# Rounded weights by a casting transfer on GpSimd's queue, in place of a multiply on GpSimd

## What is computed

```
h = rmsnorm(x, norm_w[l])
proj = jnp.einsum("bsd,de->bse", h, w_in[l])                  # 2048 -> 6160, l = 0, 1
... ssd_branch, conformer_branch, diff_attention_branch ...
x = x + jnp.einsum("bse,ed->bsd", y, w_out[l])                # 2048 -> 2048
...
z = u @ w_in                                                  # 2048 -> 9216, second block
... dilated_band_attention, hgrn2_direction, both ways ...
h = h + rmsnorm_2(y, g_post)                                  # y after @ w_out, 2048 -> 2048
gate = jax.nn.sigmoid((h @ w_pg).astype(f32))                 # 2048 -> 2048
```

## Time and profile before

| | |
|---|---|
| time, median of 3 runs | 3098.46 us (3096.57 to 3101.62) |
| span of the profiled execution | 3093.4 us |
| TensorE busy | 2997.9 us, 97% of the span |
| GpSimd busy | 1976.8 us, 64% |
| VectorE, ScalarE busy | 1750.6 us, 1000.6 us |
| bytes moved | 298.68 MB, mean 97 GB/s |

### The profile page before, as it was taken

How to read it: one execution, slowest core, us unless ns; L and a number is a source line. 1 busy time by engine, 2 the same in 40 slices (tenths; PEclk the granted TensorE clock), 3 DMA queues, 4 the chain that set the end, 5 groups by cost and what they waited for, 6 DMA issues and landing times.

```text
span 3093.4 us, 39590 instructions
## 1 busy us (share of the span) xinstructions
PE 2997.9 (97%) x15236; PEld 2355.2 (76%) x15236; DVE 1750.6 (57%) x2350; ACT 1000.6 (32%) x1712; POOL 1976.8 (64%) x1860
## 2 busy tenths in 40 slices
PE   8999999999999999999999999999999999899997
PEld 6887777788778878777877777777777777687686
DVE  7745887751374569777217443334788778801412
ACT  6243223330233331334103232233544454411422
POOL 6665676577676656756757655555567777566364
PEclk9999999999999999999999999999999999999998
DMA  5322222233223222222432222222212222232122
GB/s 210 110 102 103 82 93 84 82 142 123 99 106 109 102 86 90 97 82 75 172 109 97 84 86 70 83 72 77 79 69 83 73 80 81 93 133 98 66 89 89
DMA packets 59340, 298.68 MB, mean 97 GB/s; under 512 B 6512, under 2 KB 7408, under 8 KB 29200
## 3 DMA queue, kind: packets, MB, share of 16 engines
q1 hardware_dynamic: 36960, 251.67, 23.1%
q10 hardware_dynamic: 22192, 44.48, 4.2%
HBM read 274.04 MB, written 16.84 MB: 94 GB/s over the span
## 4 chain that ended last, share of the span: by engine, by line
PE 74%; DVE 16%; ACT 4%; POOL 3%; issue 2%; DMA 1%; ACTq 1%; DVEq 0%; POOLq 0%
PE bank L433 65%; POOL w_lo L2595 2%; DVE rec_ex L2432 1%; DVE rec_cum L2297 1%; PE bank L777 1%; POOL w_hi L2593 1%; ACT att_sc L1322 1%; PE bank L786 1%; PE bank L794 1%; DMA w_raw<-in_wall 1%; DVE newton L1796 1%; DVE newton L1798 1%; DVE bank L1899 1%; DVE att_sc L2173 1%; PE bank L966 1%
## 5 line engine op out<-in xcount | busy, mean ns | idle before, releaser
L433 PE MATMUL bank<-h_hi,w_lo 128*128 128x512 f32 x3712 | 1501.6, 405 | 24.7 <-POOL w_lo L2595 14.8
L433 PE MATMUL bank<-h_hi,w_hi 128*128 128x512 f32 x3712 | 1453.0, 391 | 0.0
L433 PE MATMUL bank<-h_lo,w_hi 128*128 128x512 f32 x3712 | 1451.5, 391 | 0.0
L2593 POOL TENSOR_SCALAR w_hi<-w_raw 128x512 fp32r<-128x512 f32 x928 | 705.3, 760 | 1004.0 <-PE bank L433 913.0
L2595 POOL TENSOR_TENSOR w_lo<-w_raw,w_hi 128x512 fp32r<-128x512 f32 x928 | 1294.0, 1394 | 77.4
L433 PEld LDWEIGHTS bank<-h_hi,w_lo 128*128 128x128 f32 x3712 | 700.6, 189 | 230.4 <-issue 52.2
L433 PEld LDWEIGHTS bank<-h_hi,w_hi 128*128 128x128 f32 x3712 | 700.1, 189 | 150.9
L433 PEld LDWEIGHTS bank<-h_lo,w_hi 128*128 128x128 f32 x3712 | 701.7, 189 | 146.2 <-issue 10.5
L1034 ACT ACTIVATE raw<-bank 128x512 f32<-128x512 f32 x148 | 88.5, 598 | 403.9 <-PE bank L433 366.3
L2098 DVE SCALAR_TENSOR_TENSOR bank<-cfm_up,par,bank 128x512 f32<-128x512 f32 x232 | 175.4, 756 | 8.3
L1805 DVE TENSOR_TENSOR sumsq<-sumsq,bank 128x512 f32<-128x512 f32 x80 | 55.0, 688 | 178.8 <-ACT bank L1718 144.7
(11 more groups left out here) (370 smaller groups left out, 2690.8 us busy)
## 6 DMA issues: line engine op xcount, KB each, us to landing
w_raw<-in_wall SPq DMA_DIRECT2D x230, 1024.0 KB, 4.9
x_scratch<-xT ACTq DMA_DIRECT2D x12, 1024.0 KB, 5.0
xT<-x_scratch ACTq DMA_DIRECT2D x12, 1024.0 KB, 8.9
ssd_abc<-acs_scratch ACTq DMA_DIRECT2D x16, 512.0 KB, 3.8
first_xin<-in_x SPq DMA_DIRECT2D x4, 1024.0 KB, 11.2
out<-last_z SPq DMA_DIRECT2D x4, 1024.0 KB, 4.1
w_raw<-in_wall SPq DMA_DIRECT2D x8, 256.0 KB, 10.2
att_tq<-att_uq ACTq DMA_DIRECT2D x32, 64.0 KB
```

What stands on the lines that cost most here:

```text
L433: mm = t.matmul(bank[BANK[u]][:, :], w[:, CS16[k]], h[:, k, :], start=(k == 0 and w is m.w_lo[b]), stop=(k == KT - 1 and w is m.w_hi[b] an ...
L2593: g.tensor_scalar(m.w_hi[b][:, part], m.w_raw[b][:, part], 1.0, 1.0, ALU.mult, ALU.mult).then_inc(*s.hi.inc(u, n))
```

## The change

For 205 of the 232 units the rounded half is no longer computed. GpSimd waits until TensorE has freed the buffers, issues one transfer of the whole unit from `in_wall` into the float32r tensor `w_hi`, which rounds on the way, waits for it and for SyncE's transfer of the same unit into `w_raw`, and then does the four subtractions alone. The 25 units of the pairs that go by quarters, and the first two units, are made as before.

```diff
+        self.cast = [signal(f"cast{b}", 16) for b in range(2)]
...
-    def split(u, n):
+    def rounded(u, n):
         b, part = u % 2, slice(n * PIECE, (n + 1) * PIECE)
         g.tensor_scalar(m.w_hi[b][:, part], m.w_raw[b][:, part], 1.0, 1.0, ALU.mult, ALU.mult).then_inc(*s.hi.inc(u, n))
         g.wait_ge(*s.hi.at(u, n))
+
+    def rest(u, n):
+        b, part = u % 2, slice(n * PIECE, (n + 1) * PIECE)
         g.tensor_tensor(m.w_lo[b][:, part], m.w_raw[b][:, part], m.w_hi[b][:, part].bitcast(F32), ALU.subtract).then_inc(
             *s.lo.inc(u, n))
+
+    def cast(u):
+        b = u % 2
+        g.dma_start(m.w_hi[b][:, :], io["wall"][u, :, :]).then_inc(*s.cast[b].inc(u))
...
         behind_pair = u - 2 in PAIRED or u - 2 in OUT_PAIR
+        by_quarters = behind_pair or u - 1 in OUT_PAIR
         us = (u, u + 1) if u in PAIRED or behind_pair else (u,)
-        for b in us:
-            g.wait_ge(*s.raw[b % 2].at(b))
+        if by_quarters:
+            for b in us:
+                g.wait_ge(*s.raw[b % 2].at(b))
+        else:
+            g.wait_ge(*s.unit.at(us[-1] - 2))
+            for b in us:
+                cast(b)
+            for b in us:
+                g.wait_ge(*s.raw[b % 2].at(b))
+                g.wait_ge(*s.cast[b % 2].at(b))
         for n in range(PIECES):
...
             for b in us:
-                split(b, n)
+                if by_quarters:
+                    rounded(b, n)
+                rest(b, n)
```

More of the change, by code:

```diff
@@ L2585, in vector_engine, with pool_engine @@
     last()
-def pool_engine(nc, m, s):
+def pool_engine(nc, io, m, s):
     g = nc.gpsimd
-    def split(u, n):
+    def rounded(u, n):
         b, part = u % 2, slice(n * PIECE, (n + 1) * PIECE)
@@ L2600, in pool_engine @@
             g.wait_ge(*s.piece[u][n].at("w"))
-            split(u, n)
+            rounded(u, n)
+            rest(u, n)
     u = 2
@@ L2612, in pool_engine @@
                 g.wait_ge(*s.pe.at("read", OUT_PAIR[u - 1], n))
-            elif n == 0 or behind_pair or u - 1 in OUT_PAIR:
+            elif by_quarters:
                 g.wait_ge(*s.unit.at(us[-1] - 2))
             for b in us:
-                split(b, n)
+                if by_quarters:
+                    rounded(b, n)
+                rest(b, n)
         u += len(us)
@@ L2641, in build @@
         sync_engine(nc, io, m, s)
-        pool_engine(nc, m, s)
+        pool_engine(nc, io, m, s)
         tensor_engine(nc, m, s)
```

## The result

The changed kernel takes 3264.12 us (median of 4 runs, 3257.71 to 3271.73) against 3099.05 before: a ratio of 1.0535, 95% interval 1.0523 to 1.0548, 165 us slower. The profiled execution took 3271.73 us with a span of 3269.9, so that only 1.8 us lie around a span; of the 5.1 us that the prediction put there most was the spread between executions.

A forecast was written before the change was run, and what follows sets the result against it. TensorE, busy 97%, bounds the kernel; GpSimd has 3.0 us per unit to spare. Terms 87 + 40 + 29 + 10 - 10 + 13 = 169 us on 3098.5 give about 3270 us, range 3150 to 3660.

The forecast's parts named there:

- P = X + 4 s, nothing overlapping: GpSimd's cycle per unit: X from freed buffer to landed transfer, s one subtraction; 13.2 us in the output products.
- quick case: GpSimd's transfer colliding with SyncE's raw one: X = 4.9 + 2.5 = 7.4 us, data time from full slices' 415 GB/s.
- the slow one: Same collision of two transfers, with 3.4 us of data time added: X = 4.9 + 3.4 = 8.3 us.
- 10 us of lead: Entering six dense stretches, GpSimd's first quarter is ready at 9.3 us, wanted at 10.9: 6 x 1.6 = -10 us.
- dense terms: Stretches where TensorE does only units: output products 87 us, conformer 40, gate 29, each P less TensorE's interval.
- The whole pair: Units ("wo", l, 14) and 15: two transfers land before two subtractions, 10.6 us in place of 4.1; +6.5 each, +13.
- ssd branch: Both layers, some 32 units at P less 12.65 us: 18 us at most, about 10 left for uneven intervals.
- The clock: TensorE's 1.2 GHz level returns in places after waits of some 2 us per unit; costed at nothing.
- The slow transfer: Rival, chance 0.22: type-changing transfer at half the raw rate, X = 10.3 to 11, +550, 3650 us.
- The late description: Rival, chance 0.16: VectorE delays GpSimd's transfer description 2 us more than the collision hides; X = 9.2, +300, 3400 us.
- The hidden transfer: Rival, chance 0.03: X stays under 5.7, TensorE pays only at the pairs (+8) and little else; 3100 to 3110 us.
- the gain: Rival "faster", chance 0.04: X near 4.9, GpSimd gives VectorE its port for 623 us more; more likely 15 us, 3083.

The follow-up runs named there:

- the run of subtractions alone: Changed kernel without casting transfer and multiplies for the 205 units, GpSimd only waiting and subtracting, w_hi keeping older weights: 3084.57 us, ratio 0.9953 to the kernel before.
- the plain transfer: Changed kernel without raw transfers for the 205 units, GpSimd's transfer plain float32 into w_raw instead of casting into w_hi: 3131.15 us, ratio 1.0106 to the kernel before.

## Why the prediction was right

It forecast 3270 us and 3264 came. Its steps, in their order:

*The bound and its margin.* Right. TensorE bound, GpSimd with 3.0 us to spare, and the price wherever the new cycle exceeds TensorE's interval. The run with transfers in the second block's mixers alone shows the condition by itself (3097.99 for 3096.01). The prediction counts the 820 multiplies at the mean of all 928, 623 us; by rows they took 599 (705.3 for all, 106.0 for the 108 that stay in the run of subtractions alone), which changes nothing in the sum.

*P = X + 4 s, nothing overlapping.* Right: 12.58 us, of which X 7.6 and 4 s 5.0, predicted 8.0 and 5.2. Its quick case, 7.4, was the nearer; the slow one rests on "nine full slices" of the earlier trace rows, of which only five are above 300 GB/s. The collision is the whole difference between 7.6 and 5.3, and the reason given for it (both queues released at one moment) was shown by delaying one of them. The description on GpSimd shows up as 0.58 us; alone, its transfer lands in 5.3 where SyncE's took 4.9.

*The sum.* The mechanism held everywhere, sizes did not. On the profiled spans, which are 176.5 us apart for the 169 predicted, each as measured and as predicted: output products 19.7 (first layer), 15 (second) and 19.4 (second block), 54 for 87; conformer 2 x 16.3, 33 for 40; gate 19.4 for 29. P was taken 0.6 too long, over 69 units some 40 us too much; with the 10 us of lead that the prediction took off again the dense terms are 40 too high. The whole pair was predicted at +6.5 and took 34.3 us for 27.1, +7.2; TensorE's wait at its start is this row of the trace after, and no second wait follows:

```profile
885.95 0.77 PE L434 MATMUL bank<-h_hi,w_lo 128*128 128x512 f32 x1 [9.50 <-POOL w_lo L2599]
```

It replaces the 2.30 and 0.91 us of the earlier trace rows, 6.3 us more.

In the ssd branch 10 us were allowed. It lost 11.0 in 12 units of the first layer alone, and some 24 in all; the prediction named its uneven intervals and took off for them, where they seem to add: at 12.6 us a unit, even intervals of 12.65 would have lost nothing.

*The term that was missing.* The output pair at the start of each product: unit `("wo", l, 0)` is now made by a transfer, and GpSimd comes to the quarters of `("wo", l, 1)` behind it, while TensorE wants both. 31.0 us for 21.7, and about as much in the second layer, +18 in all. What stands behind the new wait on GpSimd was asked for the pairs made whole and not for this one. Attention, which had no term in the sum either, took 14 us more in its two parts. These 32 us and the 14 more of the ssd branch have the size of the excess in the dense terms. That the total came within 6 us (8 on the spans) is thus in part luck: the terms for the dense stretches were 40 us too high together, and others too low or missing by 46.

*The clock.* 0.85 and 0.89 were granted in the stretches with the longest waits and 0.97 to 1.00 in the dense ones, so 1.2 GHz came back in places, as said. That it costs nothing where GpSimd sets the cycle was argued, and no run separates it. In the whole pair, where TensorE has to catch up, it did cost something: the matmuls right behind the wait of 9.50 us start 0.43 us apart, 0.23 in the dense stretch at 2.4 GHz, and of the 7.2 us that the pair lost 6.3 are waiting.

*The rivals.* The slow transfer (0.22): out, by the plain transfer and by 5.3 us alone. The Trainium skill ("DMA: Bandwidth & Descriptors", section Bandwidth) gives 6.15 us of busy DMA engines for 1 MB from GpSimd. That was not met: from issue to landing there are 5.3 us in all. The late description (0.16): out as well; the 205 transfers of the run with the raw ones delayed land in 5.0 at the least and 5.3 in the median. VectorE and GpSimd do hold each other up, by the computing operations. The hidden transfer and the gain: with the collision and the serial order gone 4.6 us are gained, of the 15 that the prediction allowed, and 14 with the transfers left out. Its reason for a gain, VectorE less held up, fits what the recurrent part shows in that run; TensorE's waits for `w_lo` fell there by 4.0 us.

*What the profile would show.* 12.6 for 13.2 us a cycle, 1.4 to 1.6 us of wait for each unit for "about 2", the banded part untouched, 214.97 MB more, all as described. Raw transfers land in 5.8, not 7: they are ahead, and GpSimd's pays more of the collision. GpSimd's busy time is 1492 us, not 1300: 104 us of multiplies at the units made as before and 118 us of issues count, which the estimate left out.

## What to carry to other kernels

An engine that works in order and both issues a transfer and uses it has a cycle of landing plus work; compare that sum with the interval of the engine it feeds, stretch by stretch, not its busy time, which fell here while the kernel got 5% slower. When two queues are released by one event, their transfers collide each time; a wait on the queue that has slack was the cheapest cure here (3130 us with this one edit). Issuing ahead of the last pieces of work shortens the cycle too, but alone it was worse here (3155 and 3181 us), as the pieces then stood where they held up VectorE; it won only with a wait between the pieces and the pairs left as they were (3093 us). Work taken from an engine that is not the bound is worth what others waited for it, here 14 us of some 600, and a version that leaves it out altogether measures that first.

## What the runs showed of the hardware

- GpSimd's subtractions without waits between them hold back a VectorE operation with two inputs in SBUF for all of them: 4.53 us behind three and 3.3 behind two, in place of 0.75; with a wait behind each of three the median is 1.8. In the kernel before, which waits between multiply and subtraction, it was 0.87 and at most 1.56.
- A transfer of 1 MB from GpSimd's queue costs it 0.57 us to issue and lands in 5.3 us, 0.3 to 0.4 behind SyncE's, and rounding float32 to float32r on the way adds nothing.
- Two transfers of 1 MB issued together land after 5.8 and 7.5 us; in the window shown the DMA slices then stand at 410 to 437 GB/s.
